# VectorE's step in four attentions: the low half of a turned block moved ahead of the next mask and inverse

## The reference

```python
s = jnp.einsum('bqhgd,bkhd->bhgqk', qb, kb).astype(jnp.float32) * scale
s = jnp.where(mask, s, -jnp.inf)
p = jax.nn.softmax(s, axis=-1)          # swa: the sum has one more term, a sink logit of the head
return jnp.einsum('bhgqk,bkhd->bqhgd', p.astype(v.dtype), vb)
```

## Time and profile before

| | |
|---|---|
| median of 3 runs | 3077.32 us (3075.08 to 3079.61) |
| profiled execution | 3074.39 us, span 3072.6 us, mean granted TensorE clock 0.912 |
| busy: PE, PEld | 2735.6 us (89%), 2163.7 us (70%) |
| busy: DVE, ACT, POOL | 1396.4 us (45%), 794.2 us (26%), 1767.5 us (58%) |

### The profile page before, as it was taken

The page is one execution under the profiler, slowest core; times in us unless marked ns, Lnnn a source line. Parts: engine busy times, 40 slices in busy tenths (PEclk is TensorE's granted clock), DMA queues, the critical chain, the costliest instruction groups (busy, mean ns, idle before and its releaser), DMA issues. The chain is left out here.

```text
span 3072.6 us, 38015 instructions
## 1 busy us (share of the span) xinstructions
PE 2735.6 (89%) x12010; PEld 2163.7 (70%) x12010; DVE 1396.4 (45%) x2919; ACT 794.2 (26%) x1725; POOL 1767.5 (58%) x1019
## 2 busy tenths in 40 slices
PE   5889778789999987889999899998899898899998
PEld 3677556557888756658888577776687776687876
DVE  6337666624344157732111346666215734352452
ACT  3200566622111134531111322222103612200001
POOL 3426333346777635437777454443477876587773
PEclk9779787899999986589999899999899999999999
DMA  5427000024565210123333221111142222233332
GB/s 214 124 94 210 29 1 1 1 61 144 159 208 173 83 41 28 38 68 89 96 96 96 62 90 55 55 55 48 48 108 76 55 84 89 76 96 89 89 92 65
DMA packets 420978, 260.08 MB, mean 85 GB/s; under 512 B 62893, under 2 KB 411434, under 8 KB 414322
## 3 DMA queue, kind: packets, MB, share of 16 engines
q1 hardware_dynamic: 390368, 193.18, 21.7%
q10 hardware_dynamic: 30481, 65.31, 6.3%
HBM read 254.25 MB, written 8.10 MB: 85 GB/s over the span
## 5 line engine op out<-in xcount | busy, mean ns | idle before, releaser
L563 POOL TENSOR_TENSOR W<-RAW,zeros 128x1024 fp32r<-128x1024 f32 (+2 forms) x355 | 680.7, 1917 | 964.4 <-PE PA L631 736.7
L570 POOL TENSOR_TENSOR W<-RAW,W 128x1024 fp32r<-128x1024 f32 (+2 forms) x355 | 852.4, 2401 | 33.8 <-PE PA L635 7.4
L630 PE MATMUL PA<-H,W 128*128 128x512 f32 x1408 | 580.2, 412 | 55.3 <-DVE H L1437 42.7
L631 PE MATMUL PA<-H,W 128*128 128x512 f32 x1408 | 562.8, 400 | 0.0
L630 PE MATMUL PA<-A,W 128*128 128x512 f32 x944 | 378.7, 401 | 39.1 <-DVEq L1353 24.3
L630 PEld LDWEIGHTS PA<-H,W 128*128 128x128 f32 x1408 | 271.4, 193 | 150.7 <-issue 51.7
L631 PE MATMUL PA<-A,W 128*128 128x512 f32 x944 | 376.3, 399 | 0.0
L635 PE MATMUL PA<-H,W 128*128 128x512 f32 x1408 | 354.7, 395 | 0.0
L631 PEld LDWEIGHTS PA<-H,W 128*128 128x128 f32 x1408 | 273.4, 194 | 57.7 <-issue 4.6
L635 PEld LDWEIGHTS PA<-H,W 128*128 128x128 f32 x1408 | 269.8, 192 | 57.3
L630 PEld LDWEIGHTS PA<-A,W 128*128 128x128 f32 x944 | 183.0, 194 | 81.5 <-issue 42.7
(11 more groups left out here) (295 smaller groups left out, 3856.7 us busy)
## 6 DMA issues: line engine op xcount, KB each, us to landing
AD<-in_ada_w_dram ACTq DMA_DIRECT2D x40, 1024.0 KB, 5.2
RAW<-in_w_in_dram SPq DMA_DIRECT2D x160, 256.0 KB, 3.2
RAW<-in_mlp_w_up_dram SPq DMA_DIRECT2D x128, 256.0 KB, 3.1
RAW<-in_mlp_w_down_dram SPq DMA_DIRECT2D x128, 256.0 KB, 3.0
RAW<-in_w_up_dram SPq DMA_DIRECT2D x88, 256.0 KB, 3.1
RAW<-in_nsa_w_in_dram SPq DMA_DIRECT2D x40, 256.0 KB, 3.9
RAW<-in_w_down_dram SPq DMA_DIRECT2D x16, 384.0 KB, 3.7
RAW<-in_swa_w_in_dram SPq DMA_DIRECT2D x20, 256.0 KB, 3.3
```

The lines of the kernel that those rows point to most:

```text
L563: e.tensor_tensor(W[0][:, s, 0:kc], RAW[:, s, 0:kc], zeros[:, 0:1].rearrange("p (a b) -> p a b", b=1).broadcast_to([P, kc, P]), ALU.add).t ...
L570: e.tensor_tensor(W[1][:, s, 0:kc], RAW[:, s, 0:kc], W[0][:, s, 0:kc].bitcast(F32), ALU.subtract).then_inc(w_split, 1)
L630: pe.matmul(PA[s][:, 0:n], W[0][:, s, k], hi, start=(k == 0), stop=False)
L631: mm = pe.matmul(PA[s][:, 0:n], W[0][:, s, k], lo, start=False, stop=False)
```

## The change

In `attention` of DVE the part that makes the low half is written ahead of the mask and of the inverse of the same step. It is the same instruction with the same waits; only its place in DVE's order is another. The loops of PE, ACT, POOL and SP are unchanged.

```diff
                         last = dve.tensor_tensor(dst, src, hi.bitcast(F32), ALU.subtract)
                     last.then_inc(sem("split_lo"), 1)
+                if plan.lo <= i < n + plan.lo:
+
+                    j = i - plan.lo
+                    G, b, u = j // 4, j % 4, u0 + j
+                    grp = plan.groups[G]
+                    blocks = (grp["keys"][b] + P - 1) // P
+                    row = G % plan.ring * plan.blocks + grp["at"][b]
+                    part = [x[0:grp["rows"], row:row + blocks, qcols(b)] for x in plan.turned]
+                    dve.wait_ge(sem("pt_hi"), u + 1)
+                    dve.tensor_tensor(part[1], plan.turn_banks[j % len(plan.turn_banks)][0:grp["rows"], 0:blocks * P].rearrange("p (a n) -> p a n", a=blocks),
+                                      part[0].bitcast(F32), ALU.subtract).then_inc(sem("pt_lo"), 1)
                 if i < n:
                     if before:
                         before(i)
...
                     dve.wait_ge(sem("exped"), u + 1)
                     dve.reciprocal(stat[3][:, u % 8:u % 8 + 1], stat[2][:, u % 8:u % 8 + 1]).then_inc(sem("inverted"), 1)
-                if plan.lo <= i < n + plan.lo:
-
-                    j = i - plan.lo
...
-                    dve.wait_ge(sem("pt_hi"), u + 1)
-                    dve.tensor_tensor(part[1], plan.turn_banks[j % len(plan.turn_banks)][0:grp["rows"], 0:blocks * P].rearrange("p (a n) -> p a n", a=blocks),
-                                      part[0].bitcast(F32), ALU.subtract).then_inc(sem("pt_lo"), 1)
                 if i > plan.out and (i - plan.out) % 4 == 1:
```

## The result

The changed kernel takes 3190.5 us (median of 4 runs, 3187.7 to 3192.8) against 3078.5 us (4 runs, 3075.1 to 3080.6) for the kernel before: a ratio of 1.0373, 95% interval 1.0359 to 1.0387. The prediction was 3171 us in a range of 3127 to 3200. The profiled execution took 3192.8 us, at a mean granted clock of 0.892 in place of 0.912.

A forecast was written before the change was run, and what follows sets the result against it. No engine is full in nsa, where engines wait for each other; PE is nearly full in swa, na and ca. Terms 63 (nsa) + 21 (swa) + 10 (na) + 0 (ca) = +94 us gave 3171 us, range 3127 to 3200.

The forecast's parts named there:

- The chain mask, exponential, high half, low half: On DVE and ACT these four follow one another in every step; in nsa 184 steps of 1.64 us take 301.8 us.
- the term for PE's product: At the end of an nsa head PE's product with the values adds 0.9 us, counted for 10 of 15 heads, 9 us.
- The term for keys and values: In nsa, splits of new keys and values in three heads add some 2.8 us a head, 8 us.
- That for the sum of the halves: In nsa, about 0.2 us in each head where this sum doesn't fit into ACT's time, 3 us.
- swa, +22.6 for +21: In swa 56 steps of 2.0 us were to take 112 us, making the window 21 us longer, between 14 and 24.
- na, +13.4 for +10: In na a head was to take 13.5 us for 12.0, seven heads +10 us, bounds 0 and 16.
- ca, +0.5 for 0: In ca PE's panel matmuls were to hide the later masks: 0 us, upper end 6.
- PE's wait for the low half is nearly gone: Sign expected in the changed profile: PE's transposes, 51.6 us of waiting before, would hardly wait for the low half.
- (a): Rival: the bank freed earlier lets PE's transposes start earlier, returning 51.6 us of waiting: 3026 us, chance 0.04.
- (b): Rival: only part shows; nsa pays 42 to 50 us and the others little, about 3127 us, chance 0.10.
- (c): Rival: nothing happens, DVE waits for ACT where it waited for PE, 3077 us, chance 0.03.
- (d): Rival: PE stays at its lower clock, slowing nsa, swa and the projections behind beyond the bounds, about 3215 us, chance 0.04.

The follow-up runs named there:

- Kernels 2: Changed kernel, with ACT's high half written ahead of the exponential of the same step in nsa and swa: 3052.5 us, 0.993 of the kernel before.
- Kernel 6: Changed kernel with ACT's high half ahead of the exponential in nsa and swa, and the earlier DVE order in na and ca: 3035.4 us, 0.987.
- kernel 3: Against the changed kernel, DVE's low half moved past the inverse alone (mask, low half, inverse): 3076.8 us, 1.000 of the kernel before.
- kernel 10: The changed kernel run and profiled once more, nothing else altered: 3186.6 us, 1.035 of the kernel before.
- kernel 4: Against the changed kernel, DVE's inverse written at the very front (inverse, low half, mask): 3196.6 us, 1.040 of the kernel before.
- kernel 8: Changed kernel with PE's transposes of three steps ahead of the product in each nsa head done three times: 3182.4 us, 1.034.

## Why the prediction was right, and where it was off

**The mechanism held.** The chain mask, exponential, high half, low half, said to close in every step, is the one in the timeline; DVE's idle time moved to the high half (236 us, 17 before; the prediction only said 80 or more), the mask starts 0.1 us ahead of the end of a low half, and the steps by width hold to 0.04 us. Kernels 2 and 6 take one link out and the loss is gone; kernel 3 leaves the mask ahead and there is none.

**nsa, +72.1 for +63: the term for PE's product was mis-sized.** From the mask of unit 7 on 184 steps took 332.0 us. The chain alone, 301.8 us, is confirmed by the steps above. The term for keys and values, 8 us, measured 7.7: three heads of 23.3 to 23.9 us for 21.1. That for the sum of the halves, 3 us, measured 2.3: the eleventh step, in which it stands, is 0.13 to 0.18 us longer than its price in each of 15 heads. The failing term is "that leaves 0.9 us ... I count it for 10 of 15 heads, 9 us". It measured 1.3 us, 1.0 in one head, and came in every one of the 15: 20 us. That is more than the 13.5 us that my upper bound has for it, and the window stayed below 76 only because other reserves in that bound weren't used. (Nor does the bound come out of its parts: 41.9 + 13.5 + 2 x 8 + 6 is 77.4.) The price of 0.9 was too low because its row was that of a PE that came to the product at the upper level, as above. The choice of 10 heads could have been refuted from the trace of before: there the product takes 2.59 us in 7 of 15 heads, 2.1 to 2.5 in 7, and 1.47, the upper level throughout, in one. With the change it takes 2.59 in 14 and 2.45 in one, at a mean granted clock of 0.72 for 0.82. Nor is it half as long at the upper level, as the prediction had it; 1.47 is 0.57 of 2.59. 301.8 + 20 + 7.7 + 2.3 = 331.8 us, of the 332.0 measured. Three heads with a third step of 2.16 in place of 1.7 us, which I hadn't counted (+1.4), are nearly made up for by other steps a few hundredths shorter than their price.

**swa, +22.6 for +21.** 56 steps of 2.03 us for 2.0. At 0.51 PE's clock is as in the earlier trace rows; the chain and not PE sets the step.

**na, +13.4 for +10: two ends weren't counted.** Heads take 13.4 to 13.65 us for the predicted 13.5. I counted seven heads at 1.5 us. Measured are six whole heads (81.4 us for 71.7, +9.7), the first one (12.85 us for 11.16, +1.7) and the last three steps, which I left out (8.00 for 5.96, +2.0).

**ca, +0.5 for 0.** The cover held: PE is busy in 55.6 of 59.3 us.

**One sign was wrong.** "PE's wait for the low half is nearly gone" is the opposite of what happened. The two places of L747, 40.3 + 11.3 = 51.6 us in the earlier trace rows, are now, from the view of the low half's line (who waited for it: us, times):

```profile
  PE PT L747: 97.1, 110
  PE PA L747: 28.8, 44
```

125.9 us. The low half stands earlier in DVE's order but not earlier in time: it is the end of a chain, and PE, which has less to do for each microsecond, stands at the bank and waits. Kernel 6, whose windows of nsa and swa are together 42 us shorter than before, has 43.8 + 9.8 = 53.6 us of this wait, no less than before. This wait is no measure of what the order is worth, in either direction.

**The rivals.** (a), the freed bank, 3026 us, falls with its mechanism: the wait that it was to return doubled. Its time is nearly that of kernel 6, but by another way, the overlap of mask with high half and exponential with low half. The rule beside it, in the Trainium skill, "Perfetto Trace Analysis", section "Optimization Strategy", is to make the dependency of the blocked engine start sooner. Read as an earlier place in the order, it led to a loss of 3.7% here: PE was blocked by the low half, and the earlier place didn't start it sooner. (b) falls with nsa at +72 and swa at +23, (c) with all of it. (d) had the clock right in direction (0.82 to 0.72 in nsa) but not its price: nsa and swa stay below my upper bounds of 76 and 24 us, and between and behind the attentions there are 3 us in all, not 10.

**What is left.** The windows account for 108.6 of the 118.4 us between the two spans, most of the rest for the execution, as kernel 10 shows. By its windows the prediction was 14.6 us short, by its medians 16 to 20.

## What to carry to other kernels

On an engine that works in order, an instruction that is written earlier takes its wait along, and everything behind it waits too: before moving one, look at what stands ahead of its producer on the other engine, and whether that needs something which would now be queued behind the moved instruction. If it does, two engines that overlapped take turns, and the step becomes the sum of their links, which can be read from the timeline to a few hundredths of a microsecond. Don't turn DVE's order without ACT's: here DVE's move alone costs 3.7%, ACT's alone gives 0.7%, and both together, kept to the two attentions that have them, 1.3%.

## What the runs showed of the hardware

**A split on DVE that lasts four times as long beside one on POOL.** In kernel 4, in na, the split of the next q starts within 0.02 us of a weight split on POOL (start, length, engine, line):

```profile
2519.05 2.34 POOL L570 TENSOR_TENSOR W<-RAW,W 128x1024 fp32r<-128x1024 f32 x1
2519.07 2.87 DVE L1458 TENSOR_TENSOR QS<-QN,QS 64x512 fp32r<-64x512 f32 x1
2521.97 0.68 DVE L1458 TENSOR_TENSOR KK0l<-KN,KK0h 64x512 fp32r<-64x512 f32 x1
```

It ends 0.55 us behind POOL's, and takes 2.87 us where all eight of the changed kernel take 0.69. It happens in each of the six whole heads (2.86 to 2.94 us), which take 15.2 to 15.5 us in place of 13.5, and is kernel 4's +10 us in na. Both have two operands in SBUF. In the changed kernel the same split starts 0.07 us ahead of another operation of POOL, the product with the inverse:

```profile
2468.31 0.69 DVE L1458 TENSOR_TENSOR QS<-QN,QS 64x512 fp32r<-64x512 f32 x1
2468.38 2.05 POOL L588 TENSOR_SCALAR pr<-pr,stat_inv 128x512 f32<-128x512 f32 x1 [0.60 <-DVE stat_inv L1492]
2469.03 1.76 DVE L1458 TENSOR_TENSOR KK0l<-KN,KK0h 64x512 fp32r<-64x512 f32 x2
```

Here DVE's first split keeps its 0.69 us, POOL's operation takes 2.05 us, where the one ahead of it has 1.56, and the two splits of k take 0.88 us each in place of 0.69. The Trainium skill, "Perfetto Trace Analysis", section "Optimizing Scalar/DVE Operations", says that GpSimd and DVE share a read port of SBUF, and both rows agree with that. Kernel 4's row looks as if DVE had waited for the whole of POOL's operation; the other row shows both going on, each somewhat longer. No run changed the operands or the order of the starts alone, so which property of the two operations decides between these stays open. For orders like these it means that an edit that costs nothing by its own waits can still cost by the moment at which it puts an operation beside POOL's.

**A product at either level of the clock in one kernel.** The same eight matmuls took 2.59 us (granted clock 0.50, the lower level, 1.2 GHz) in a PE with pauses and 1.47 us (1.00) in kernel 8, where more transposes came ahead of them. The mean granted clock of nsa was 0.91 where it took 235 us, 0.86 at 243, 0.82 at 269 and 0.72 at 341 (0.69 when the changed kernel was profiled again), and 0.78 at 342 us in kernel 8, with more matmuls in the same time. So here a slower chain on DVE and ACT came with a slower PE, and kernel 8 shows that PE's pauses, and not the length of the stage, go with it; the one place where PE still sets the step grew.
